# Seven block products in place of eight in the gated feed-forward down projections, with block sums made by DVE and GpSimd

## The reference

```python
def swiglu(x, w_in, w_out):
    a, b = jnp.split(x @ w_in, 2, axis=-1)
    return (jax.nn.silu(a) * b) @ w_out

h = h + 0.5 * swiglu(rmsnorm(h, ffn1_norm[l]), ffn1_w_in[l], ffn1_w_out[l])
...
h = h + 0.5 * swiglu(rmsnorm(h, ffn2_norm[l]), ffn2_w_in[l], ffn2_w_out[l])
```

## Time and profile before

| | |
|---|---|
| median of 3 runs | 1388.68 us (1388.59 to 1388.95) |
| profiled execution | 1388.56 us, span on the core 1386.8 us |
| granted PE clock, mean | 0.999 of full speed |
| first gated stage, first ordinary up chunk to last down matmul | 510.16 to 682.17 us |
| second gated stage, the same | 1208.63 to 1380.64 us |
| bytes read from HBM | 225.90 MB, 164 GB/s over the span |

### The profile page before, as it was taken

The page is one execution under the profiler, slowest core; times in us unless marked ns, Lnnn a source line. Parts: engine busy times, 40 slices in busy tenths (PEclk is TensorE's granted clock), DMA queues, the critical chain, the costliest instruction groups (busy, mean ns, idle before and its releaser), DMA issues.

```text
span 1386.8 us, 25234 instructions
## 1 busy us (share of the span) xinstructions
PE 1366.7 (99%) x9092; PEld 1238.9 (89%) x9092; DVE 1026.2 (74%) x1601; ACT 803.9 (58%) x1310; POOL 24.2 (2%) x71
## 2 busy tenths in 40 slices
PE   8999999999999999999999999999999999999998
PEld 8999999988888888888899989989989898888887
DVE  5786787677666686666788888888888877666665
ACT  4445554644343354444678898898898844544443
POOL 6000000000000000000000000000000000000000
PEclk9999999999999999999999999999999999999999
DMA  8565554556555746566564535535434276566661
GB/s 265 149 191 150 144 149 156 187 188 205 182 185 195 228 137 197 182 183 201 151 164 134 140 106 148 137 95 157 130 105 143 79 196 212 153 203 197 198 190 61
DMA packets 298383, 227.82 MB, mean 164 GB/s; under 512 B 10882, under 2 KB 280404, under 8 KB 298324
## 3 DMA queue, kind: packets, MB, share of 16 engines
q1 hardware_dynamic: 298324, 227.01, 55.0%
HBM read 225.90 MB, written 1.08 MB: 164 GB/s over the span
## 4 chain that ended last, share of the span: by engine, by line
PE 88%; DVE 6%; DVEq 3%; issue 2%; ACT 1%; DMA 0%; ACTq 0%
PE G L1968 7%; PE G L1970 7%; PE G L1969 7%; PE M L1985 7%; PE M L1973 7%; PE G L1985 7%; PE M L1974 7%; PE M L1975 7%; PE G L1987 4%; PE M L1987 4%; DVEq L1152 3%; PE G L2691 2%; PE G L1973 2%; PE G L1975 2%; PE G L1974 2%; PE G L2088 2%
## 5 line engine op out<-in xcount | busy, mean ns | idle before, releaser
L1155 DVE TENSOR_TENSOR w_lo<-w_raw,w_hi 128x2048 fp32r<-128x2048 f32 (+2 forms) x249 | 481.2, 1936 | 155.9 <-ACT w_hi L624 152.7
L624 ACT ACTIVATE w_hi<-w_raw 128x2048 fp32r<-128x2048 f32 x198 | 378.0, 1910 | 173.3 <-PE G L1970 75.0
L1968 PE MATMUL G<-xa,w_hi 128*128 128x256 f32 x992 | 294.9, 297 | 0.0
L1970 PE MATMUL G<-xa,w_lo 128*128 128x256 f32 x992 | 280.3, 283 | 0.0
L1969 PE MATMUL G<-xa,w_hi 128*128 128x256 f32 x992 | 280.1, 282 | 0.0
L1968 PEld LDWEIGHTS G<-xa,w_hi 128*128 128x128 f32 x992 | 189.4, 191 | 3.6 <-issue 2.2
L1969 PEld LDWEIGHTS G<-xa,w_hi 128*128 128x128 f32 x992 | 189.5, 191 | 1.7 <-issue 1.7
L1970 PEld LDWEIGHTS G<-xa,w_lo 128*128 128x128 f32 x992 | 189.1, 191 | 0.0
L1973 PE MATMUL M<-w_hi,xb 128*128 128x512 f32 x304 | 119.0, 391 | 0.6 <-DVE xb L1155 0.5
L1974 PE MATMUL M<-w_lo,xb 128*128 128x512 f32 x304 | 118.7, 390 | 0.0
L1975 PE MATMUL M<-w_hi,xb 128*128 128x512 f32 x304 | 118.3, 389 | 0.0
(11 more groups left out here) (401 smaller groups left out, 2520.1 us busy)
## 6 DMA issues: line engine op xcount, KB each, us to landing
w_raw<-in_w_in SPq DMA_DIRECT2D x150, 512.0 KB, 4.8
w_raw<-in_ffn_w_in SPq DMA_DIRECT2D x88, 512.0 KB, 5.0
w_raw<-in_w_ff SPq DMA_DIRECT2D x64, 512.0 KB, 4.2
w_raw<-in_ffn_w_out SPq DMA_DIRECT2D x44, 512.0 KB, 4.7
w_raw<-in_w_in SPq DMA_DIRECT2D x33, 256.0 KB, 3.3
w_raw<-in_w_out SPq DMA_DIRECT2D x16, 512.0 KB, 4.1
w_raw<-in_w_branch_gdn SPq DMA_DIRECT2D x16, 512.0 KB, 5.1
w_raw<-in_w_branch SPq DMA_DIRECT2D x12, 512.0 KB, 4.2
```

What stands on the lines that cost most here:

```text
L624: nc.scalar.activation(w_hi[:, slot, :], w_raw[:, slot, :], ACT.Copy).then_inc(hi_ready, 1)
L1155: return v.tensor_tensor(dst, src, hi.bitcast(F32), ALU.subtract)
L1968: mm(out_, w[0], x[0], start=first, stop=False)
L1970: return mm(out_, w[1], x[0], start=False, stop=last_)
```

## The change

Nine of the eleven down chunks of each gated stage are computed as a 2 x 2 block product by Strassen's algorithm (in Winograd's form): seven products of blocks of 128 x 128 by 128 x 512 in place of eight. Each product keeps its own accumulator bank over all nine chunks: M[3], M[0], M[1], M[2], M[4], M[5] and G[1] for products 1 to 7. The combination of the seven is made once for a stage, on DVE, into the residual `res`. What the scheme needs:

- Weight sums: three sums of the quarters of the raw down chunk (`t_raw`), and the second quarter is replaced by a difference in the raw buffer itself. DVE makes them in four operations (`weight_sums`), ACT the high part (`wsums_hi`) and DVE the low part (`weight_sums_low`), over 1536 columns.
- Activation sums: four sums of the blocks of two hidden tiles, 128 columns each, made by GpSimd (`s_raw`), with high part by ACT (`sums_hi`) and low part by DVE (`hidden_sums_low`), over 512 columns.
- Banks: M[4], M[5] and G[1] are accumulators now, so all up chunks use `col_gemm`, and, but for the second ordinary one and the last, all of them bank G[0]. The reductions go; Silu and product read the bank directly.
- Order: on PE a down chunk's products follow one period later, between the next two up chunks and behind them. The last two down chunks stay as before, on top of the accumulators.
- Three semaphores elsewhere are merged with others; they count the same events.

The diff, cut to what matters for the time. The first `period` in it is ACT's, the second DVE's, the third PE's; chunk `c` there is the first up chunk of the period, `c + 2` the down chunk whose products PE runs in it:

```diff
+        for f in range(2):
+            for pair in range(SEVENS):
+                pool.wait_ge(ffn_step, (STEPS + 1) * f + 2 * pair + 3)
+                done(nc.gpsimd.tensor_tensor(s1, a21, a22, ALU.add))
+                done(nc.gpsimd.tensor_tensor(s3, a11, a21, ALU.subtract))
+                settle()
+                done(nc.gpsimd.tensor_tensor(s2, s1, a11, ALU.subtract))
+                settle()
+                done(nc.gpsimd.tensor_tensor(s4, a12, s2, ALU.subtract))
...
+            def sums_hi(r_, pair):
+                act.wait_ge(built, BUILT_ALL + 4 * (SEVENS * f + 1) + pair * 4)
+                nc.scalar.activation(xb_hi[:, sums_of_pair(r_), :].rearrange("p k t -> p (k t)"), s_raw, ACT.Copy
+                                     ).then_inc(hh_ready, 1)
+
+            def wsums_hi(down):
+                act.wait_ge(wsum_ready, SEVENS * f + down + 1)
+                nc.scalar.activation(t_hi, t_raw, ACT.Copy).then_inc(wsum_hi, 1)
+
+            def period(k, i=0, bank=0):
+                c, r_, kk = c0 - 1 + 3 * k, k % 2, k + i * 2
+                silu(c + 1 + i * 6, 0, 0)
+                split(c + RING, i, 6)
+                hidden_hi(r_, 0, 2 * kk)
+                if k <= 8 and bank == 0:
+                    act.wait_ge(wsum_used, SEVENS * f + kk)
+                    wsums_hi(kk)
+                silu(c + 2 + i * 6, 1, bank)
+                split(c + 1 + RING, i, 6)
+                hidden_hi(r_, 1, 2 * kk + 1)
+                if k <= 8 and bank == 1:
+                    act.wait_ge(wsum_used, SEVENS * f + kk)
+                    wsums_hi(kk)
+                split(c + 2 + RING, i, 6)
+                if k <= 8:
+                    sums_hi(r_, kk)
...
             for n in range(2):
                 first_silu(n)
-                split(c0 + n + RING)
+                if n == 0:
+                    split(c0 + RING)
                 first_hi(n)
-            with act.Fori(0, 4) as i:
-                steps(i)
-            steps(4, True)
+            wsums_hi(0)
+            split(c0 + 1 + RING)
+            sums_hi(0, 0)
+            period(1, 0, 1)
...
+            def weight_sums(base, i=0):
+                slot = base % RING
+                dve.wait_ge(w_loaded[slot], loads(base) + i * (loads(base + 6) - loads(base)))
+                q = quarters(w_raw, slot)
+                v.tensor_tensor(t_raw[:, 1, :], q[:, 3, :], q[:, 1, :], ALU.subtract)
+                v.tensor_tensor(q[:, 1, :], q[:, 1, :], q[:, 0, :], ALU.subtract)
+                settle()
+                v.tensor_tensor(t_raw[:, 0, :], t_raw[:, 1, :], q[:, 0, :], ALU.add)
+                settle()
+                v.tensor_tensor(t_raw[:, 2, :], q[:, 2, :], t_raw[:, 0, :], ALU.subtract).then_inc(wsum_ready, 1)
...
+            def period(k, i=0, bank=0):
+                c, r_, kk = c0 - 1 + 3 * k, k % 2, k + i * 2
+                hh = h0 + 3 * k + i * 6
+                product(0, 0, 2 * kk)
+                w_low(c + RING, i, 6)
+                hidden_low(r_, 0, hh + 1)
+                if k <= 8:
+                    weight_sums(c + 2 + RING, i)
+                product(1, bank, 2 * kk + 1)
+                if k <= 8 and bank == 0:
+                    weight_sums_low(kk)
+                w_low(c + 1 + RING, i, 6)
+                hidden_low(r_, 1, hh + 2)
+                if k <= 8 and bank == 1:
+                    weight_sums_low(kk)
+                if k <= 8:
+                    hidden_sums_low(r_, hh + 3)
+                    w_low(c + 2 + RING, i, 6)
...
+            weight_sums(c0 + 4)
+            weight_sums_low(0)
+            hidden_sums_low(0, h0 + 3)
             w_low(c0 + 4)
-            with dve.Fori(0, 4) as i:
-                steps(i)
-            steps(4)
+            period(1, 0, 1)
+            with dve.Fori(0, 3) as i:
+                period(2, i)
+                period(3, i)
+            period(8)
+            period(9)
+
+            dve.wait_ge(gemm_done, c0 + 29)
+            p1, p5, p6, p7 = M[:, 3, :], M[:, 4, :], M[:, 5, :], G[:, 1, :]
+            left, right = drained
+            v.tensor_copy(left, p1)
+            into(0, 0, p1)
+            settle()
+            half_sum(left, p6)
+            settle()
+            v.tensor_tensor(right, left, p7, ALU.add)
+            v.drain().then_inc(evac[1], 1)
+            w_low(c0 + 31)
+            product(0, 0, 20)
+            half_sum(left, p5)
+            into(1, 0, right)
+            settle()
+            half_sum(right, p5)
+            into(0, 512, left)
+            settle()
+            into(1, 512, right)
+            w_low(c0 + 32)
+            hidden_low(0, 0, h0 + h_count(20))
+            product(1, 1, 21)
+            hidden_low(0, 1, h0 + h_count(21))
+            w_low(c0 + 33)
...
+        def seven(c, r_, products, first=False, last=False):
...
+            table = {1: (M[:, 3, :], a(0, 0), q(0)), 2: (M[:, 0, :], a(1, 0), q(2)), 3: (M[:, 1, :], s(3), q(3)),
+                     4: (M[:, 2, :], a(1, 1), t(2)), 5: (M[:, 4, :], s(0), q(1)), 6: (M[:, 5, :], s(1), t(0)),
+                     7: (G[:, 1, :], s(2), t(1))}
+            for n in products:
+                ins = three_x(*table[n], first, last and n not in (2, 3, 4))
+            return ins
...
+            def from_sums(c, pair, i=0, first=False, last=False):
+                r_, n = pair % 2, pair + i * 2
+                pe.wait_ge(wsum_lo, SEVENS * f + n + 1)
+                pe.wait_ge(h_ready, h0 + 3 * pair + 2 + i * 6)
+                seven(c, r_, (4,), first, last)
+                pe.wait_ge(h_ready, h0 + 3 * pair + 3 + i * 6)
+                seven(c, r_, (6,), first, last)
+                if first:
+                    pe.wait_ge(evac[1], ev[1] + 2)
+                seven(c, r_, (7,), first, last).then_inc(wsum_used, 1)
+
+            def period(k, i=0, last=False):
+                c, kk = c0 - 1 + 3 * k, k + i * 2
+                up(c, i, 0, ev[0] - 2 + 2 * kk)
+                from_sums(c + 2, k - 1, i, False, last)
+                weights_ready(c + 2 + i * 6)
+                seven(c + 2, (k - 1) % 2, (1,), False, last)
+                up(c + 1, i, 0, ev[0] - 1 + 2 * kk)
+                seven(c + 2, (k - 1) % 2, (2, 5, 3), False, last).then_inc(gemm_done, 1)
...
+            up(c0 + 2, 0, 0, ev[0] + 1, lambda: turn(1))
+            up(c0 + 3, 0, 1, ev[1] + 1)
+            from_sums(c0 + 4, 0, 0, True)
+            weights_ready(c0 + 4)
+            seven(c0 + 4, 0, (1, 2, 5, 3), True).then_inc(gemm_done, 1)
+            with pe.Fori(0, 3) as i:
+                period(2, i)
+                period(3, i)
+            period(8)
+            period(9, 0, True)
+            up(c0 + 29, 0, 0, ev[0] + 2 * SEVENS)
+            up(c0 + 30, 0, 1, ev[1] + 3)
```

More of the change, by code:

```diff
@@ L232, in emit @@
     fin_row = rows[:, 0, :]
+    t_hi, t_lo = (grid(part[:, 8:14, :].rearrange("p k t -> p (k t)"), n=3, c=512) for part in (xb_hi, xb_lo))
+    t_raw = grid(tmp.rearrange("p i d -> p (i d)")[:, 0:3 * 512], n=3, c=512)
+    s_raw = ffs[:, 1, :]
+    drained = [ffr[:, n, :] for n in range(2)]
     gain1, gain_mix, gain2 = mrg, mrg2, mrg
@@ L824, in first_hi @@
             def first_hi(n):
[L825 to L837, removed]
@@ L839, in steps @@
-            def steps(i, final=False):
-                for u in range(2):
-                    c = c0 + 2 + 3 * u
-                    for n in range(2):
-                        hidden(c + n + (i * 6 if final else 0), 0 if final else i, 6, n, h0 + 2 + 2 * u + n + i * 4,
-                               (1 + u) % 2 * 2 + n, final and u == 1 and n == 1)
-                    if not (final and u == 1):
-                        split(c + 2 + RING, i, 6)
+                act.wait_ge(turned, 3 + 2 * f + n)
@@ new lines, in first_hi, with silu, hidden_hi @@
+                nc.scalar.activation(xb_hi[:, n, :], M[:, 4 + n, 0:T], ACT.Copy).then_inc(hh_ready, 1)
+            def silu(c, n, bank):
+                act.wait_ge(gemm_done, c)
+                nc.scalar.activation(ffn_s[:, n, :], G[:, bank, 0:T], ACT.Silu).then_inc(ffr_ready, 1)
+            def hidden_hi(r_, n, tile):
+                act.wait_ge(ffn_step, (STEPS + 1) * f + tile + 2)
+                nc.scalar.activation(xb_hi[:, 4 * r_ + n, :], ffn_h[:, n, :], ACT.Copy).then_inc(hh_ready, 1)
@@ L855, in ffn @@
+            period(8)
+            period(9)
+            for n in range(2):
+                silu(c0 + 30 + n, n, n)
+                hidden_hi(0, n, 20 + n)
+                split(c0 + 29 + n + RING)
             log_exp_set()
@@ L1567, in steps @@
[L1567 to L1575 removed]
+                low_of(xb_lo[:, n, :], M[:, 4 + n, 0:T], xb_hi[:, n, :]).then_inc(h_ready, 1)
@@ L1577, in ffn, with half_sum, into @@
+            def half_sum(out_, bank):
+                return v.tensor_tensor(out_, out_, bank, ALU.add)
+            def into(i, lo_, y):
+                x = res[:, i, lo_:lo_ + 512]
```

(13 more changed lines are left out.)

158 lines of the change are left out of this document (82 added, 76 removed).

## The result

The changed kernel takes 1454.57 us (1451.42 to 1457.26) where the kernel before takes 1388.78 in the same series: a ratio of 1.0474, 95% interval 1.0462 to 1.0487. It is slower, as forecast, by 66 us; forecast were 72. The profiled execution took 1456.6 us, its span 1454.9. Its page: busy us of each engine, the tenths of PE and the granted clock in 40 slices, and the chain that ended last by engine.

The account below looks back on a forecast made before the run. PE's own issue rate was taken to bound the kernel, so every added wait is paid in full. 1388.6 us before, plus 69.2 for two stages 34.6 longer each, plus 3 for the clock: 1461 us, range 1430 to 1486.

Parts of the forecast that it names:

- its arithmetic saves 5.3: PE's matmul time over both stages: 12.3 us less from dropped products, 7.0 us back from narrower ones, net 5.3 less.
- narrow chunks: 38 up chunks in both stages become 256-column matmuls, 5.76 us against 5.58 each: 7.0 us more in all.
- The loop: Each later period: a closed six-step chain of load, weight sums, copy, Silu and product, GpSimd's sums, last low parts: 20.05 us.
- shared turn: Step 5 of the chain: GpSimd's four sums interleave with three DVE low parts, 5.63 us with exclusion.
- GpSimd and DVE exclude each other: Two-input operations of both engines can't overlap, less some 0.15 us start-up: period 20.05 us, against 18.35 without.
- Rival A: GpSimd runs beside DVE without exclusion: periods of 18.35 us, each stage 22.4 more, total 1436 us; chance 0.20.
- The head: Each stage's first pair: the seventh product waits 10.5 us for tile 3's product on DVE and starts at 23.9.
- The clock: PE's clock falls to 1.2 GHz in the head's wait: 1.5 us a stage taken, between nothing and 3.4.
- The first round: Each stage from its first ordinary up chunk until the chain first closes: 33.1 us.
- The rest of a stage: PE's work after seven rounds: remaining products, up chunks, matmul groups and waits of 0.6 and 1.6: 33.1 us.
- Rival C: Weights land sooner, so the load is outside the chain; PE's 16.3 us decides: about 1396 us; chance 0.04.
- Rival D: PE never waits and only the arithmetic is left: 1383 us; a loss above 2.7 us of waits a stage; chance 0.04.

Follow-up runs that it names:

- the kernel with the constants: Changed kernel with GpSimd writing constants in place of its four activation-block sums, so products 3, 5, 6 and 7 take wrong operands: 1434.13 us.
- the exchange: Changed kernel with DVE's product of the second pair's second tile put ahead of the next up residual, load wait and weight sums: 1446.77 us.
- the idle products at the head: Changed kernel with idle 512-column products on PE ahead of the wait for the first seventh product's bank: 22 took 1464.61 us, 11 took 1445.86 us.
- the load's own buffers: Changed kernel with the nine summed down chunks loaded into two raw buffers of their own, a whole turn ahead: 1420.61 us.
- the kernels with everything together: Changed kernel with own down buffers, new head order, Silu before weight-sum copy, last collected sums behind the last product: 1401.17 us; also with GpSimd constants: 1392.41 us.
- DVE's block sums: The four activation-block sums made by DVE, not GpSimd, in the kernel with the four things done together: 1395.39 us, ratio 1.0050 to the kernel before.

## Why the prediction was right

- **PE sets the end; its arithmetic saves 5.3.** Held in its parts: turns need 16.32 (said: 16.3), narrow chunks cost 3.5 a stage as said. The 5.3 themselves were seen in no run.
- **The loop.** Right in each of its six steps, and the order of the waits is the one foretold. Sizes in the undisturbed turn, said and measured: low part done to first sum 5.24 and 4.87 (564.69 to 569.56); sums 3.10 and 2.84; copy 1.52 and 1.42; Silu and product .88 and .82; shared turn 5.63 and 5.54; the rest 3.68 and 3.59. Together 20.05 and 19.08. Outside the load .6 a turn was too much, nearly half of it in the sums: behind a drain they start .77 apart and not .86. The load was read from one row. In this turn it is .37 shorter than said; over the fourteen turns, counted the same way, it is 4.75 to 6.85 and 5.37 on the mean. That 5.24 lies so near is luck. Seven turns were to take 140.4 and took 135.3 and 139.5, 6 us less in all.
- **GpSimd and DVE exclude each other.** Held, and this was the step with the thinnest rows. Rival A said 1436 for no exclusion; the kernel with the constants took 1434.13. (By the rival's own steps its first round is 31.4 and not 32.8, and its time some 3 us less.) A sum on 128 columns takes .46 us where .40 was assumed. The Trainium skill ("SBUF — State Buffer", SBUF: two separate sides) calls this pair an exclusive lock; the turn above agrees, with 1.98 and 2.39 in place of .46. Its figure in "GPSIMD Engine Reference", Performance versus the Vector engine, scaled down, is an estimated .28 us and a start, which .46 does not contradict.
- **The head.** The seventh product was said to start at 23.9 after a wait of 10.5; it started at 22.8 after 9.5 (23.2 and 9.9 in the second stage). The cause, DVE's queue order, was shown by the exchange.
- **The clock.** The term that was mis-sized: 1.5 us a stage were taken, and the idle products at the head give back 2.8 and 3.2. The upper bound on record, 3.4 for the 15 matmuls behind the wait at half clock, was the right reading: 15 starts .427 apart in place of .229 are 3.0 us more.
- **The first round** was to close at 33.1 and 1.5 for the clock; it closed at 34.8 and 35.3. With the idle products it closes at 31.9 and 32.1. So it was 1.1 too long without the clock and the clock some 1.5 too short: two errors that cancel, which is luck.
- **The rest of a stage**, 33.1: measured 33.19 and 33.18.

Added up, a stage is 34.8 + 135.3 + 33.2 = 203.3 and 35.3 + 139.5 + 33.2 = 208.0, against 34.6 + 140.4 + 33.1 = 208.1 as forecast. The first stage is 4.8 below, the second meets it, and that is because its loads happened to land later (5.42 on the mean from issue to first sum, 4.84 in the first). The point on record looks better than its terms.

Rival C (load not in the loop) fell with the load's own buffers, which took 34 us away. Rival D was put to the test by the kernels with everything together: with DVE's block sums PE never waits in a turn, and 3.6 us of waits a stage are left, against the 2.7 at which the gain was said to turn: .5% slower than before.

## What to carry to other kernels

Saving one of eight products buys nothing unless the operands of the other seven are made off the chain: here 12 us of matmuls were saved (by the count on record), 7 went into narrower chunks, and the head and the loop of load, sums, copies and a shared turn cost 71 more. When a change adds a step that consumes a load, follow the buffer round once: who frees it, who issues, who waits; a chain that closes on itself sets the period whatever the busy shares say. Then try the orders: exchanging two ACT instructions gave back 24 us, raw buffers of the down chunks' own 34. And where a load stands in a loop, take its time from many rows: here it made nearly all of the spread between turns.

## What the runs showed of the hardware

- A GpSimd operation with two operands that starts within a DVE one with two operands ends .32 us behind it (1.98 and 2.39 us in place of .46), and DVE loses too: 1.76 became 1.94 and 2.29 became 2.55, while four constants written by GpSimd cost DVE nothing.
- The clock falls to its lower level within a wait of 9.5 us and stays there some 6 us into the work behind it. Idle products through the wait keep it at full. In turns of the changed kernel with a wait of 1.8 to 3.5 us for the bank the mean granted clock is .91 or .92, in those with at most 1.6 us it is 1.00; a wait of 1.80 in the kernel with 11 idle products left it at 1.00.
- A load of 1 MB, issued in two parts, took 4.51 to 6.61 us from issue to its first reader in like turns of one execution. The turn outside it stayed within .1 us.
- A product of 512 columns with operands of full float32 leaves two records and takes .87 us; the kernel's own, in its reduced form, start .23 apart.
- A wait of .3 us stood in no list of waits and showed only in the distance of two starts.
